# A shared SBUF region that starts at a multiple of 512 bytes instead of 64

## The chip, the core and the metric

The kernel runs on one core of a Trainium2 chip. What is measured is the time of one execution on the device, in microseconds (us).

## What is computed

Two transformer-like blocks on a 512 x 1024 float32 activation. The first has a gated MLP branch, an HGRN2 branch and a feed-forward layer; the second has two layers, each with a SwiGLU feed-forward, a mixer (attention with a pooling branch, then a short convolution) and another SwiGLU. Cut to what the change touches:

```python
x = x + mix @ w_out[l]
h = rmsnorm(x, norm_ffn[l])
x = x + jnp.square(jax.nn.relu(h @ w_ff1[l])) @ w_ff2[l]
...
mod = (c_act @ w_ada[l] + b_ada[l]).reshape(b, N_MOD, 1, D_MODEL)
...
def swiglu(h, wg, wu, wd):
    return (jax.nn.silu(h @ wg) * (h @ wu)) @ wd
```

## The kernel before

The activation is kept transposed in SBUF (`xT`, features on the 128 partitions, 512 tokens along the free dimension). Every large product runs in units of 256 output columns: SyncE loads a 1 MB panel of float32 weights into `w_raw`, ScalarE rounds it to float32r in `w_hi`, VectorE takes the rest into `w_lo`, all three with two slots. The moving operand is also split in two. Outputs of norms are in `a_hi` and `a_lo`; the hidden activations that go into a "down" product (and the mixers' outputs) are in `b_hi` and `b_lo`; the two branches of the first block leave theirs in `c_hi`, `c_lo` and `d_hi`, `d_lo`. The inner loop of such a product, the function `product`, issues three matmuls for each 128 x 128 block of weights (L622, L623, L624 in the profile), each with 512 float32r columns of the moving operand:

```python
pe.matmul(o, wh, hi[:, k, :], start=(k == ks[0]), stop=False)
pe.matmul(o, wh, lo[:, k, :], start=False, stop=False)
mm = pe.matmul(o, wl, hi[:, k, :], start=False, stop=(k == ks[-1]))
```

The function is called with `a_hi, a_lo`, with `b_hi, b_lo` (by `down` and by `hidden_group`), and with the c and d pairs (by `branches`). In the names of the profile the moving operand stands first: `po<-b_hi,w_hi` streams `b_hi` past weights from `w_hi`.

The program places every tensor by hand. `sb` gives the next free address of each partition, rounded up to 32 bytes; as the program is built, the first tensor, `xT`, is at byte 16512. The tensors that live through the whole program come first. Behind the last of them, `level_mask`, begins the region that the stages share, called `arena`. `ar` places a tensor at the arena's start plus a whole number of KB:

```python
def ar(name, shape, dt, kb):
    return sb(name, shape, dt, arena + kb * KB)
c_hi = ar("c_hi", [P, DK, S], F32R, 0)
b_hi = ar("b_hi", [P, DK, S], F32R, 48)
b_lo = ar("b_lo", [P, DK, S], F32R, 64)
```

In the arena are the b, c and d pairs, all working tensors of the HGRN2, gated MLP, attention and convolution stages (`cum`, `kk`, `qq`, `de`, `ql`, `kl`, `gv`, `qk`, `pr`, `cv` and others), the input `x_in`, and `ada_in` and `ada_acc`, which hold rows of w_ada and their running sum in the feed-forward stage of the first block. Outside it are `xT`, `w_raw`, `w_hi`, `w_lo`, `a_hi`, `a_lo`, `sq`, `stats`, `nt`, `ev`, `hid` and small tensors; the large ones of these all start at a remainder of 128 when their byte address is divided by 512.

The remainders that matter later, from adding up the sizes in the code (bytes within a partition):

| tensor | address before | mod 512 | mod 128 | address of the change | mod 512 | mod 128 |
|---|---|---|---|---|---|---|
| w_hi | 49280 | 128 | 0 | 49280 | 128 | 0 |
| a_hi | 82048 | 128 | 0 | 82048 | 128 | 0 |
| arena, c_hi | 144832 | 448 | 64 | 144896 | 0 | 0 |
| b_hi | 193984 | 448 | 64 | 194048 | 0 | 0 |
| b_lo | 210368 | 448 | 64 | 210432 | 0 | 0 |

`hi[:, k, :]` and each 128-column block of weights step in multiples of 512 bytes from the tensor's start, so a matmul's operand has the remainder of its tensor.

Each engine has its own instruction stream, and semaphores alone order them. In the feed-forward stage of the first block (`hidden_group`) VectorE also sums `ada_in` times `c_act` into `ada_acc` (L1729, L1732), squares the hidden activations into `hid` (L1764), makes `b_lo` (L1768), and adds each finished down unit to `xT` (L1777).

Of the kernel before, what the change touches and what calls it, by code (L numbers as in the profile page):

```python
# [51 lines left out]
def hybrid_two_block_kernel(  # L52
# [58 lines left out]
    with ctx:  # L111

        cursor = [(nc.sbuf_usable_end - nc.sbuf_bytes_remaining + 31) // 32 * 32]

        def sb(name, shape, dt, offset=None):
            size = {F32: 4, F32R: 4, I32: 4, U8: 1}[dt]
            for n in shape[1:]:
                size *= n
            if offset is None:
                offset = cursor[0]  # L120
                cursor[0] = (offset + size + 31) // 32 * 32
            return nc.alloc_sbuf_tensor_at(name, shape, dt, offset=offset)
# [28 lines left out]
        one_col = sb("one_col", [P, 1], F32)  # L151
        small = sb("small", [P, 64], F32)
        level_mask = sb("level_mask", [P, LV + 1, P], U8)
        arena = cursor[0]
        KB = 1024

        def ar(name, shape, dt, kb):
# [1863 lines left out]
```

## Time and profile before

| | |
|---|---|
| median of 3 runs | 2880.39 us (2879.53 to 2882.75) |
| the profiled execution, its own time | 2878.74 us |
| its span | 2876.6 us |
| TensorE (PE) busy | 2747.4 us, 96% |
| VectorE (DVE) busy | 1435.5 us, 50% |
| ScalarE (ACT) busy | 929.1 us, 32% |
| moved from and to HBM | 112 GB/s over the span |

The span is the time between the first and the last instruction of the profile. Busy times of TensorE add up matmuls whose ends are modelled and overlap; the distance between the starts of two matmuls in the timeline is the better measure of their pace.

### The profile page before, as it was taken

How to read it: one execution, taken by the hardware profiler on the slowest of the kernel's cores; microseconds unless marked ns; L12 is line 12 of the kernel's file. 1: busy time of each engine (PE TensorE's matmuls, PEld its weight loads, DVE VectorE, ACT ScalarE, POOL GpSimd, SP SyncE). 2: the span in 40 equal slices, each digit the busy share in tenths (PEclk: the TensorE clock that was granted, in tenths of full speed). 3: DMA queues.
4: the chain of work that ended last, by engine and by line, in shares of the span. 5: the costliest groups of instructions: out<-in, count | busy, mean ns of one | idle time of the engine just before them, and what ended most of it. 6: DMA issues, size and time to landing. Idle time of an engine off the chain costs nothing.

```text
span 2876.6 us, 32115 instructions
## 1 busy us (share of the span) xinstructions
PE 2747.4 (96%) x12573; PEld 2255.2 (78%) x12573; DVE 1435.5 (50%) x1561; ACT 929.1 (32%) x1087; POOL 29.0 (1%) x50
## 2 busy tenths in 40 slices
PE   7999999999999699999968999999999999999998
PEld 6888878778777488887846788887888878788887
DVE  6677553488889733325264433344333454533333
ACT  4555423332222332224343322134222332332221
POOL 0000000000000000000030000000000000000000
PEclk9999999999999899999979999999999999999999
DMA  4111222377778233232311232322323222233322
GB/s 133 60 58 59 66 88 85 97 281 278 289 297 303 85 102 95 95 99 77 100 38 44 88 102 88 102 88 88 102 88 103 88 93 97 75 104 99 102 88 73
DMA packets 252092, 323.43 MB, mean 112 GB/s; under 512 B 5622, under 2 KB 242420, under 8 KB 243828
## 3 DMA queue, kind: packets, MB, share of 16 engines
q1 hardware_dynamic: 240740, 245.51, 26.6%
q10 hardware_dynamic: 11280, 76.94, 6.8%
q8 instruction: 47, 0.77, 0.1%
q14 instruction: 25, 0.20, 0.0%
HBM read 320.34 MB, written 2.10 MB: 112 GB/s over the span
## 4 chain that ended last, share of the span: by engine, by line
PE 84%; DVE 10%; issue 2%; ACT 2%; DMA 1%; ACTq 0%; SPq 0%; DVEq 0%
PE po L622 22%; PE po L624 21%; PE po L623 21%; PE po L596 3%; PE po L601 3%; PE po L597 3%; DVE w_lo L1379 2%; DVE ada_acc L1732 2%; PE pm L742 2%; PE po L705 1%; PE po L707 1%; PE po L706 1%; DVE ada_tr L1741 1%; PE pm L655 1%; DMA ada_in<-in_w_ada_dram 1%
## 5 line engine op out<-in xcount | busy, mean ns | idle before, releaser
L1379 DVE TENSOR_TENSOR w_lo<-w_raw,w_hi 128x1024 fp32r<-128x1024 f32 x472 | 561.9, 1220 | 503.2 <-ACT w_hi L970 503.1
L970 ACT ACTIVATE w_hi<-w_raw 128x1024 fp32r<-128x1024 f32 x472 | 479.1, 1051 | 900.1 <-PE po L624 871.5
L622 PE MATMUL po<-a_hi,w_hi 128*128 128x512 f32 x1792 | 700.7, 391 | 4.1 <-DVE w_lo L1379 4.1
L624 PE MATMUL po<-a_hi,w_lo 128*128 128x512 f32 x1792 | 698.4, 390 | 0.0
L623 PE MATMUL po<-a_lo,w_hi 128*128 128x512 f32 x1792 | 698.3, 390 | 0.0
L622 PE MATMUL po<-b_hi,w_hi 128*128 128x512 f32 x1152 | 457.2, 397 | 16.8 <-DVE b_lo L1768 15.1
L624 PE MATMUL po<-b_hi,w_lo 128*128 128x512 f32 x1152 | 453.8, 394 | 0.0
L623 PE MATMUL po<-b_lo,w_hi 128*128 128x512 f32 x1152 | 451.1, 392 | 0.0
L622 PEld LDWEIGHTS po<-a_hi,w_hi 128*128 128x128 f32 x1792 | 337.1, 188 | 75.5 <-DVE w_lo L1379 4.9
L623 PEld LDWEIGHTS po<-a_lo,w_hi 128*128 128x128 f32 x1792 | 337.2, 188 | 70.7 <-issue 0.7
L624 PEld LDWEIGHTS po<-a_hi,w_lo 128*128 128x128 f32 x1792 | 337.1, 188 | 70.6
L622 PEld LDWEIGHTS po<-b_hi,w_hi 128*128 128x128 f32 x1152 | 218.3, 190 | 64.8 <-DVE b_lo L1768 16.8
L624 PEld LDWEIGHTS po<-b_hi,w_lo 128*128 128x128 f32 x1152 | 217.9, 189 | 50.7
L623 PEld LDWEIGHTS po<-b_lo,w_hi 128*128 128x128 f32 x1152 | 218.2, 189 | 48.1
L1445 DVE SCALAR_TENSOR_TENSOR xT<-po,gate,xT 128x512 f32<-128x512 f32 x112 | 81.5, 748 | 297.8 <-PE po L624 297.8
L1822 DVE TENSOR_TENSOR hid<-ev,po 128x1024 f32<-128x1024 f32 x44 | 53.7, 1221 | 274.8 <-PE po L624 274.8
L596 PE MATMUL po<-a_hi,w_hi 128*128 128x512 f32 x336 | 136.1, 405 | 24.5 <-ACT a_hi L1000 24.5
L1732 DVE SCALAR_TENSOR_TENSOR ada_acc<-ada_in,c_act,ada_acc 128x2304 f32<-128x2304 f32 x56 | 144.1, 2611 | 1.9 <-DMA ada_in<-in_w_ada_dram 1.9
L597 PE MATMUL po<-a_hi,w_lo 128*128 128x512 f32 x336 | 135.4, 403 | 0.0
L1257 ACT ACTIVATE ev<-po 128x1024 f32<-128x1024 f32 x44 | 45.2, 1027 | 217.9 <-PE po L624 217.7
L601 PE MATMUL po<-a_lo,w_hi 128*128 128x512 f32 x336 | 107.7, 403 | 0.8 <-DVE a_lo L1415 0.8
L596 PEld LDWEIGHTS po<-a_hi,w_hi 128*128 128x128 f32 x336 | 66.0, 196 | 45.0 <-issue 30.9
(251 smaller groups left out, 2469.5 us busy)
## 6 DMA issues: line engine op xcount, KB each, us to landing
ada_in<-in_w_ada_dram ACTq DMA_DIRECT2D x64, 1152.0 KB, 5.7
w_raw<-in_ffn_wg_dram SPq DMA_DIRECT2D x44, 1024.0 KB, 5.3
w_raw<-in_ffn_wu_dram SPq DMA_DIRECT2D x44, 1024.0 KB, 5.3
w_raw<-in_w_ff_dram SPq DMA_DIRECT2D x32, 1024.0 KB, 5.3
w_raw<-in_ffn_wd_dram SPq DMA_DIRECT2D x32, 1024.0 KB, 5.1
w_raw<-in_w_in_dram SPq DMA_DIRECT2D x28, 1024.0 KB, 5.1
w_raw<-in_ffn_wd_dram SPq DMA_DIRECT2D x16, 768.0 KB, 4.7
w_raw<-in_w_in_c_dram SPq DMA_DIRECT2D x12, 1024.0 KB, 5.1
```

Of the source, the lines that this page charges most:

```text
L596: pe.matmul(po[:, slot, b, :], w_hi[:, slot, c], hi[:, k, :], start=(k == 0), stop=False)
L597: pe.matmul(po[:, slot, b, :], w_lo[:, slot, c], hi[:, k, :], start=False, stop=False)
L601: mm = pe.matmul(po[:, slot, b, :], w_hi[:, slot, c], lo[:, k, :], start=False, stop=(k == kc - 1))
L622: pe.matmul(o, wh, hi[:, k, :], start=(k == ks[0]), stop=False)
L623: pe.matmul(o, wh, lo[:, k, :], start=False, stop=False)
L624: mm = pe.matmul(o, wl, hi[:, k, :], start=False, stop=(k == ks[-1]))
L742: mm = pe.matmul(out_v[:, t, :], ks, qs, start=True, stop=True)
L970: act.activation(w_hi[:, s, part], w_raw[:, s, part], ACT.Copy).then_inc(hi_done, 1)
L1379: dve.tensor_tensor(w_lo[:, s, part], w_raw[:, s, part], w_hi[:, s, part].bitcast(F32), ALU.subtract).then_inc(lo_done, 1)
L1445: ins = dve.scalar_tensor_tensor(xT[:, c, :], po[:, s, b, :], gates[:, c:c + 1], xT[:, c, :], ALU.mult, ALU.add)
L1732: ins = dve.scalar_tensor_tensor(ada_acc[:, l, :], ada_in[:, l, :], c_act[:, k:k + 1], ada_acc[:, l, :], ALU.mult, ALU.add)
L1822: dve.tensor_tensor(hid[:, :], ev[:, 0, :], po[:, 1, :, :].rearrange("p b n -> p (b n)"), ALU.mult).then_inc(out_taken[1], 2)
```

## The change

The arena's start is rounded up to a multiple of 512 bytes. It moves from 144832 to 144896, so each tensor in it moves by 64 bytes, and no tensor outside it moves. Every engine has the same instructions in the same order as before.

```diff
         small = sb("small", [P, 64], F32)
         level_mask = sb("level_mask", [P, LV + 1, P], U8)
-        arena = cursor[0]
+        LINE = 512
+        arena = (cursor[0] + LINE - 1) // LINE * LINE
         KB = 1024
```

## Rows read from the trace of the kernel before

**Rows 1.** The page: span, and busy time of each engine.
```profile
span 2876.6 us, 32115 instructions
...
PE 2747.4 (96%) x12573; PEld 2255.2 (78%) x12573; DVE 1435.5 (50%) x1561; ACT 929.1 (32%) x1087; POOL 29.0 (1%) x50
```

**Rows 2.** The page: engines' shares of the chain that ended last.
```profile
PE 84%; DVE 10%; issue 2%; ACT 2%; DMA 1%; ACTq 0%; SPq 0%; DVEq 0%
```

**Rows 3.** Groups: line, names, shapes, count | busy us, mean ns | idle before.
```profile
L622 PE MATMUL po<-a_hi,w_hi 128*128 128x512 f32 x1792 | 700.7, 391 | 4.1 <-DVE w_lo L1379 4.1
...
L622 PE MATMUL po<-b_hi,w_hi 128*128 128x512 f32 x1152 | 457.2, 397 | 16.8 <-DVE b_lo L1768 15.1 <-DVE b_lo L1913 1.7
...
L622 PE MATMUL po<-c_hi,w_hi 128*128 128x512 f32 x64 | 25.2, 394 | 0.0
...
L622 PE MATMUL po<-d_hi,w_hi 128*128 128x512 f32 x32 | 13.7, 427 | 4.7 <-DVE d_lo L1685 4.7
```

**Rows 4.** Timeline, TensorE, first and last of 240 a matmuls: start us, us.
```profile
2398.52 0.39 PE L622 MATMUL po<-a_hi,w_hi 128*128 128x512 f32 x1
...
2452.70 0.39 PE L624 MATMUL po<-a_hi,w_lo 128*128 128x512 f32 x1
```

**Rows 5.** Timeline, TensorE, first and last of 192 b matmuls.
```profile
1804.71 0.40 PE L622 MATMUL po<-b_hi,w_hi 128*128 128x512 f32 x1
...
1848.44 0.39 PE L624 MATMUL po<-b_hi,w_lo 128*128 128x512 f32 x1
```

**Rows 6.** Timeline, TensorE, first and last of 48 c matmuls.
```profile
472.85 0.40 PE L622 MATMUL po<-c_hi,w_hi 128*128 128x512 f32 x1
...
483.62 0.39 PE L624 MATMUL po<-c_hi,w_lo 128*128 128x512 f32 x1
```

**Rows 7.** L622 alone in those three stretches: length, busy (count), clock.
```profile
2398.50:2452.92 54.42, 31.12 (x80) 15.02 (x80) 1.00 0.27 90
1804.70:1848.60 43.90, 25.22 (x64) 12.00 (x64) 1.00 0.30 96
472.84:483.80 10.96, 6.31 (x16) 3.00 (x16) 1.00 0.30 96
```

**Rows 8.** Timeline, TensorE, near 355 and 730 us, while the clock is low.
```profile
354.87 0.63 PE L624 MATMUL po<-a_hi,w_lo 128*128 128x512 f32 x1
355.29 0.63 PE L622 MATMUL po<-a_hi,w_hi 128*128 128x512 f32 x1
355.72 0.63 PE L623 MATMUL po<-a_lo,w_hi 128*128 128x512 f32 x1
...
729.06 0.63 PE L622 MATMUL po<-b_hi,w_hi 128*128 128x512 f32 x1
729.49 0.63 PE L623 MATMUL po<-b_lo,w_hi 128*128 128x512 f32 x1
729.91 0.63 PE L624 MATMUL po<-b_hi,w_lo 128*128 128x512 f32 x1
```

**Rows 9.** Timeline, TensorE: products whose moving operand is 256 weight columns.
```profile
1419.78 0.28 PE L644 MATMUL po<-w_lo,a_hi 128*128 128x256 f32 x1
1419.90 0.28 PE L645 MATMUL po<-w_hi,a_lo 128*128 128x256 f32 x1
1420.02 0.28 PE L643 MATMUL po<-w_hi,a_hi 128*128 128x256 f32 x1
```

**Rows 10.** Two stretches: PE, PEld, DVE, ACT, POOL busy (count), clock, DMA, GB/s.
```profile
1595.00:1963.00 368.00, 364.92 (x1591) 299.56 (x1590) 138.36 (x137) 107.61 (x114) 0.00 (x0) 1.00 0.30 94
...
670.00:765.00 95.00, 90.91 (x397) 74.50 (x396) 81.80 (x54) 24.08 (x25) 0.00 (x0) 0.98 0.78 288
```

**Rows 11.** Timeline, TensorE and VectorE, feed-forward stage of the first block.
```profile
727.26 0.51 PE L622 MATMUL po<-b_hi,w_hi 128*128 128x512 f32 x1 [4.09 <-DVE b_lo L1768]
...
754.00 1.29 DVE L1777 TENSOR_TENSOR xT<-po,xT 128x512 f32<-128x512 f32 x2 [1.56 <-PE po L624]
...
764.89 1.29 DVE L1777 TENSOR_TENSOR xT<-po,xT 128x512 f32<-128x512 f32 x2 [2.28 <-PE po L624]
```

**Rows 12.** Groups on VectorE, outside the arena and with operands in it.
```profile
L1379 DVE TENSOR_TENSOR w_lo<-w_raw,w_hi 128x1024 fp32r<-128x1024 f32 x472 | 561.9, 1220 | 503.2 <-ACT w_hi L970 503.1
...
L1768 DVE TENSOR_TENSOR b_lo<-hid,b_hi 128x1024 fp32r<-128x1024 f32 x16 | 19.6, 1225 | 0.0
...
L1764 DVE TENSOR_TENSOR hid<-ev 128x1024 f32<-128x1024 f32 x16 | 19.6, 1225 | 27.3 <-ACT ev L1234 27.3
```

**Rows 13.** Waits of VectorE for the w_ada rows: us in total, times, longest.
```profile
DVE ada_acc L1729 <- DMA ada_in<-in_w_ada_dram: 2.1, 1, 2.1
DVE ada_acc L1732 <- DMA ada_in<-in_w_ada_dram: 1.9, 2, 1.4
```

## Prediction

> **What bounds the kernel now.** I read the page first. TensorE is busy 96% of the span [rows 1] and carries 84% of the chain that ended last [rows 2], so whatever changes the pace of its matmuls changes the end nearly one for one. The groups by line say where those matmuls are: L622 to L624 run 1792 times each on the a pair and 1152, 64 and 32 times each on the b, c and d pairs [rows 3]. The last three are in the arena, the a pair is not. They do the same work (128 x 128 weights, 512 columns), and yet the mean of one is 391 ns for a and 397 and 394 for b and c [rows 3]. That mean has a modelled end in it, so I went to the timeline and took distances between starts in unbroken stretches at the full clock.
>
> - a: 240 matmuls from 2398.52 to 2452.70 us, 54.18 / 239 = 226.7 ns each [rows 4].
> - b: 192 from 1804.71 to 1848.44, 43.73 / 191 = 229.0 ns [rows 5].
> - c: 48 from 472.85 to 483.62, 10.77 / 47 = 229.1 ns [rows 6].
>
> The counts are three times the L622 counts of the same stretches, at granted clock 1.00 in all three, with the DMA share at 0.27, 0.30 and 0.30 [rows 7]. So a matmul that streams from the arena starts 2.3 ns later than one that streams from outside. When the granted clock is at its lower level (1.2 GHz), both step by 0.43 us [rows 8]: 512 columns at 1.2 GHz are 426.7 ns, nothing is added for either. At 2.4 GHz the columns alone would be 213.3 ns; a adds 13.4 ns to that, b and c 15.7. The products with 256 moving columns step by 120 ns [rows 9], 106.7 plus 13.3. The addition is thus a fixed one for each matmul, at the full clock only, and for arena operands it is 2.3 ns larger.
>
> What distinguishes them? Not freshness: c was written long before its products, b just before, and both pay the same. Not the distance from hi to lo: 16 KB for a, b and c alike. Not the weights: the same `w_hi` and `w_lo`. What is left is the starting address: a starts at a multiple of 128 bytes (128 mod 512), b and c 64 bytes past one (448 mod 512), or else the distance between moving operand and weights (0 for a, 320 mod 512 for b and c).
>
> **The change part by part.** It removes and adds no instruction. Every arena operand moves from 448 to 0 mod 512, and so onto a multiple of 128.
>
> *Matmuls.* The affected ones are 3 x (1152 + 64 + 32) = 3744 [rows 3]. From 229.0 to a's 226.7 is 2.25 ns unrounded: 3744 x 2.25 = 8.4 us. A few dozen of them run at the low clock, and part of the d ones behind VectorE's 4.7 us of lateness [rows 3], for which I take off 0.1. That leaves 8.3 us. Where is it on the path? In the second block's feed-forwards TensorE is busy 364.9 of 368 us [rows 10], so the saving counts whole; the next thing behind a down product is the norm, which waits for it. In the first block's feed-forward the pace is shared: TensorE waits 4.09 us for `b_lo` before the down half of a group, but in that half VectorE waits for TensorE (1.56 and 2.28 us before its additions to `xT`) [rows 11], and its chain into the next group starts from the last of those. A shorter down half starts that chain earlier, so this share counts too: four groups of 192, 768 x 2.25 = 1.7 us. If it did not, the sum would be 6.6 us. Bounds for one matmul: nothing regained (0 us), or the whole 15.7 ns that stand above the columns (58.8 us), since no row shows an operand at 0 mod 512. I take the a row, the nearest: its operand too is on a 128 boundary and not on a 256 one.
>
> *VectorE and ScalarE.* A 128x1024 subtraction takes 1220 ns wholly outside the arena, 1225 with two operands in it, and 1225 for a square that is again wholly outside [rows 12]. The arena costs them nothing that I can see, so there is nothing to gain: 0 us.
>
> *DMA.* `ada_in`, `x_in` and some small tensors are landed in the arena. VectorE waits 4.0 us in all for `ada_in` [rows 13]; that bounds a gain there, and the cover for the rest is VectorE's own sums. I take 0.
>
> Sum: 8.3 us from the profiled execution's 2878.74 gives 2870.4. The median is 1.65 us above that execution, so the forecast is 2872.1 us, 0.29% faster. A measurement of this kernel can tell about 0.2% (5.8 us) from no change.
>
> **The rivals.**
>
> *No change, 18%.* The 2.3 ns belong to the distance between moving operand and weights (or to something else than the address's remainder). That distance goes from 320 to 384 mod 512 and not to 0, so the pace stays at 229.0: 2880 us, from 2878 to 2883. For it: in the trace, address and distance change together, so neither is excluded. Against it: moving columns and weights are read at different paces through a stretch, so a fixed phase between their addresses has no time at which it holds. The Trainium skill (SBUF — State Buffer, "Door 1: The DMA port swizzle") says that SBUF has 16-byte cachelines and that a penalty is paid for crossing to a new one; both starts are multiples of 16, so by that page alone nothing would change. The rows above do not agree with it, since there a and b, both multiples of 16, differ by 2.3 ns.
>
> *Much faster, 7%.* The 13.4 ns that a pays may be its own price for starting 128 bytes into a 256- or 512-byte line. Operands at 0 mod 512 would then start without it: 3744 x 15.7 = 58.8 us less, 2822 us. For it: nothing in the trace starts at 0, and the 256-column products, also at 128, pay the same. Against it: a cost that is the same for 256 and 512 columns looks just as much like that of switching to new weights.
>
> *Slower, 5%.* At 0 mod 512 the arena stream collides with the weight reads at 128 in a way that 448 did not. Place: the same 3744 matmuls. If the addition grows by as much as it was above a's, they cost 8.4 us more: 2889 us. It counts as slower from 1.6 ns a matmul (5.8 / 3744). No row speaks for it but that the pair 0 and 128 isn't in the trace.
>
> The forecast has 70%, with its own range of 2869.5 to 2875.
>
> **How the numbers follow.** The range must leave out at most 2 in 10, so it takes the forecast's case and the one without change: 2868 to 2882.5, which leaves out the two ends (12%) and a little. Faster by over 0.2%: 70% and 7%, less 3% for a forecast case that loses the shared stages and noise with them: 0.74. Within 0.2%: 18% and that 3%: 0.21. Slower: 0.05.
>
> **What would show it.** In the new trace, a b stretch of 192 matmuls should take 43.3 us from first start to last start and not 43.7, c the same pace as a, and a itself should still be at 226.7. VectorE's 1225 and 1220 ns should stand. The second block's four feed-forwards hold 2112 of the matmuls, and should give 4.7 us of the total. I am wrong if b stays at 229.0 (the remainder is not the cause), if it falls well under 226.7 (the a pair pays for its own address too), or if b is at a's pace and the span has not moved, which would mean that another engine took the time back.

## The result, and the profile after it

The changed kernel takes 2894.8 us (median of 6 runs, 2893.79 to 2896.23) against 2880.75 us for the kernel before: ratio 1.0049, 95% interval 1.0037 to 1.0061. It is 14 us slower. The prediction was 2872.1 us, 8 us faster, with a range from 2868 to 2882.5, so the time lies outside the range and on the other side. Of the runs of the kernel before that stand beside e5 to e8, one took 3115 us at a granted clock of 0.84 and is left out of the comparisons.

The page of the changed kernel, which answers to [rows 1] and [rows 2]:

```profile
span 2893.5 us, 32115 instructions
...
PE 2765.4 (96%) x12573; PEld 2256.7 (78%) x12573; DVE 1435.3 (50%) x1561; ACT 929.0 (32%) x1087; POOL 29.0 (1%) x50
...
PE 85%; DVE 10%; issue 2%; ACT 2%; DMA 1%; ACTq 0%; SPq 0%; DVEq 0%
```

TensorE alone has grown, by 18 us. VectorE and ScalarE have their old busy times to 0.2 us. The lines of the source are one further down now, so L622 is L623. Its groups in the changed kernel (columns as in [rows 3]):

```profile
L623 PE MATMUL po<-a_hi,w_hi 128*128 128x512 f32 x1792 | 700.0, 391 | 4.1 <-DVE w_lo L1380 4.1
...
L623 PE MATMUL po<-b_hi,w_hi 128*128 128x512 f32 x1152 | 460.2, 399 | 16.7 <-DVE b_lo L1769 14.7 <-DVE b_lo L1914 1.7 <-DVE w_lo L1380 0.3
...
L623 PE MATMUL po<-c_hi,w_hi 128*128 128x512 f32 x64 | 25.3, 395 | 0.0
```

The a pair stands at 391 ns as before, b has gone from 397 to 399. The timeline of the changed kernel gives the distances between starts. These are the first and the last matmul of an a stretch of 240, a b stretch of 192 and a c stretch of 48, the ones of [rows 4], [rows 5] and [rows 6]:

```profile
2412.55 0.39 PE L623 MATMUL po<-a_hi,w_hi 128*128 128x512 f32 x1
...
2466.72 0.39 PE L625 MATMUL po<-a_hi,w_lo 128*128 128x512 f32 x1
...
1815.23 0.40 PE L623 MATMUL po<-b_hi,w_hi 128*128 128x512 f32 x1
...
1859.79 0.39 PE L625 MATMUL po<-b_hi,w_lo 128*128 128x512 f32 x1
...
475.04 0.40 PE L623 MATMUL po<-c_hi,w_hi 128*128 128x512 f32 x1
...
486.00 0.39 PE L625 MATMUL po<-c_hi,w_lo 128*128 128x512 f32 x1
```

a: 54.17 / 239 = 226.7 ns, as before. b: 44.56 / 191 = 233.3 ns, and was 229.0. c: 10.96 / 47 = 233.2. So each arena matmul is about 4.3 ns slower, and 3744 x 4.3 = 16 us. That covers the 14 us of the medians; the interval of the ratio is 11 to 18 us.

Is something else touching SBUF at those moments? In the windows view of the changed kernel (columns as in [rows 10]) there is a piece of the same b stretch in which VectorE, ScalarE and GpSimd do nothing:

```profile
1841.50:1848.30 6.80, 6.80 (x31) 5.47 (x30) 0.00 (x0) 0.00 (x0) 0.00 (x0) 1.00 0.49 154
```

The matmuls inside it, from the timeline, 27 of them from first to last:

```profile
1841.82 0.40 PE L623 MATMUL po<-b_hi,w_hi 128*128 128x512 f32 x1
...
1847.89 0.40 PE L625 MATMUL po<-b_hi,w_lo 128*128 128x512 f32 x1
```

6.07 / 26 = 233.5 ns: the pace is the same with the other compute engines silent. The DMA queues are at work there (the last but one figure of the row, 0.49 of their time). In the last down product of the program they are not:

```profile
2860.00:2881.00 21.00, 21.00 (x92) 16.89 (x91) 6.22 (x8) 2.01 (x2) 0.00 (x0) 1.00 0.00 0
...
2860.22 0.40 PE L624 MATMUL po<-b_lo,w_hi 128*128 128x512 f32 x1
...
2880.99 0.39 PE L623 MATMUL po<-b_hi,w_hi 128*128 128x512 f32 x1
```

The last of these is the 90th, so 20.77 / 89 = 233.4 ns without any DMA: it is not DMA either. At the low clock level no difference shows, as before the change ([rows 8]): the step is 0.43 us.

```profile
732.77 0.63 PE L624 MATMUL po<-b_lo,w_hi 128*128 128x512 f32 x1
733.20 0.63 PE L625 MATMUL po<-b_hi,w_lo 128*128 128x512 f32 x1
733.62 0.63 PE L623 MATMUL po<-b_hi,w_hi 128*128 128x512 f32 x1
```

### The profile page after: what moved, and what is told of

Same layout as the page of the kernel before. It is cut to its first block, busy times and chain, and to the rows that moved or that the text cites. A ratio compares the mean times of both kernels' runs of the same rounds, so it can differ in the third digit from the quotient of the medians.

```text
span 2893.5 us, 32115 instructions
## 1 busy us (share of the span) xinstructions
PE 2765.4 (96%) x12573; PEld 2256.7 (78%) x12573; DVE 1435.3 (50%) x1561; ACT 929.0 (32%) x1087; POOL 29.0 (1%) x50
## 4 chain that ended last, share of the span: by engine, by line
PE 85%; DVE 10%; issue 2%; ACT 2%; DMA 1%; ACTq 0%; SPq 0%; DVEq 0%
PE po L623 22%; PE po L624 22%; PE po L625 22%; PE po L597 2%; PE po L602 2%; PE po L598 2%; PE pm L743 2%; DVE w_lo L1380 2%; DVE ada_acc L1733 2%; PE po L706 1%; PE po L708 1%; PE po L707 1%; DVE nt L1411 1%; DVE ada_tr L1742 1%; ACT ev L1235 1%
## 5 line engine op out<-in xcount | busy, mean ns | idle before, releaser
L623 PE MATMUL po<-a_hi,w_hi 128*128 128x512 f32 x1792 | 700.0, 391 | 4.1 <-DVE w_lo L1380 4.1
L623 PE MATMUL po<-b_hi,w_hi 128*128 128x512 f32 x1152 | 460.2, 399 | 16.7 <-DVE b_lo L1769 14.7
L624 PE MATMUL po<-b_lo,w_hi 128*128 128x512 f32 x1152 | 458.8, 398 | 0.0
L623 PEld LDWEIGHTS po<-a_hi,w_hi 128*128 128x128 f32 x1792 | 336.8, 188 | 76.3 <-DVE w_lo L1380 5.4
L623 PEld LDWEIGHTS po<-b_hi,w_hi 128*128 128x128 f32 x1152 | 219.0, 190 | 72.6 <-DVE b_lo L1769 16.5
```

## The experiments

Two theories stood after the result. Theory A: the operand's own address modulo 512 sets its pace (128 good, 448 middling, 0 bad). Theory R: the distance between the moving operand and the weights sets it. Below, "distance" is the address of the moving tensor less that of `w_hi`. It is 0 mod 512 for the a pair, 320 for the arena before, 384 with the change. The step or pace is always the distance between the starts of two matmuls that follow each other. All edits are against the kernel before.

**e1: everything 64 bytes further up.**

```diff
-        cursor = [(nc.sbuf_usable_end - nc.sbuf_bytes_remaining + 31) // 32 * 32]
+        cursor = [(nc.sbuf_usable_end - nc.sbuf_bytes_remaining + 31) // 32 * 32 + 64]
```

> Every tensor of the program, outside the arena too, is 64 bytes further up. The arena then starts at 0 mod 512, as in the change, and the weights and the a pair at 192; the distances between tensors are those of the kernel before. Theory A (the address of the moving operand, taken modulo 512, sets its pace): b matmuls step by 233.3 ns as in the change, and the a pair, now at 192, may leave 226.7; 2893 us or more. Theory R (the distance between moving operand and weights sets it: 0 gives 226.7, 320 gives 229.0, 384 gives 233.3): nothing moves, b at 229.0, a at 226.7, 2880.5 us.

Measured: 2879.64 us against 2880.11, ratio 0.9997 (0.9987 to 1.0006). A b stretch of 192 from its timeline:

```profile
1213.30 0.40 PE L622 MATMUL po<-b_hi,w_hi 128*128 128x512 f32 x1
...
1257.04 0.39 PE L624 MATMUL po<-b_hi,w_lo 128*128 128x512 f32 x1
```

43.74 / 191 = 229.0 ns, though the arena is at the very address that it has in the changed kernel. The a pair, now at 192 mod 512, still has 226.7. Theory A falls: neither pair pays for the address that it has here.

**e2: only the arena, to distance 0.**

```diff
-        arena = cursor[0]
+        arena = cursor[0] + 192
```

> Only the arena moves, by 192 bytes: it starts at 128 mod 512 like all large tensors outside it, so address and distance to the weights are both those of the a pair (distance 0 mod 512). Theories A and R both expect b, c and d at 226.7 ns and a median 8 us below the kernel before, near 2872 us. Theory H (what lies above some address, as 128 KB, is slower, and the low bits only change by how much): b stays above 229.

Measured: 2870.4 us (11 runs), ratio 0.9971 (0.9962 to 0.998). The b stretch:

```profile
1203.31 0.39 PE L622 MATMUL po<-b_hi,w_hi 128*128 128x512 f32 x1
...
1246.61 0.39 PE L624 MATMUL po<-b_hi,w_lo 128*128 128x512 f32 x1
```

43.30 / 191 = 226.7 ns, the pace of a. The gain that had been forecast for the change is here, at another address.

**e3 and e4: pieces of the arena at different distances.** The b, c and d pairs are each shifted by their own amount; the lists give the first KB of a piece and its shift.

```diff
+        SHIFT = [(0, 128), (32, 256), (48, 384)]      # e3
+        SHIFT = [(0, 96), (32, 320), (48, 448)]       # e4
...
-            return sb(name, shape, dt, arena + kb * KB)
+            extra = [s for first, s in SHIFT if kb >= first][-1]
+            return sb(name, shape, dt, arena + kb * KB + extra)
```

> Three pieces of the arena are shifted by different amounts: the c pair by 128 bytes (64 mod 512, distance to the weights 448), the d pair by 256 (192, distance 64), the b pair by 384 (320, distance 192). Theory R expects c to be no better than 229, since the three known distances 0, 320, 384 give 226.7, 229.0 and 233.3, and cannot say more; theory A expects the b pair, whose remainder is 64 mod 128 as before, at 229.0, and c and d, both 64 mod 128 too, at 229.0.

> Three pieces of the arena are shifted by different amounts: the c pair by 96 bytes (32 mod 512, distance to the weights 416), the d pair by 320 (256, distance 128), the b pair by 448 (384, distance 256). Theory A in the form that only a multiple of 256 is bad: d 233.3, b near 226.7. Theory R: unknown distances; if the cost grows with the distance up to a wrap, d 227 to 228, b 228 to 229, c over 233.

Measured, one execution each: 2893.23 and 2880.14 us. b stretches of 192 in e3, then in e4, and a c stretch of 48 in e4:

```profile
1211.60 0.39 PE L624 MATMUL po<-b_hi,w_hi 128*128 128x512 f32 x1
...
1256.17 0.39 PE L626 MATMUL po<-b_hi,w_lo 128*128 128x512 f32 x1
```

```profile
1210.47 0.39 PE L624 MATMUL po<-b_hi,w_hi 128*128 128x512 f32 x1
...
1253.76 0.39 PE L626 MATMUL po<-b_hi,w_lo 128*128 128x512 f32 x1
...
399.44 0.40 PE L624 MATMUL po<-c_hi,w_hi 128*128 128x512 f32 x1
...
410.44 0.40 PE L626 MATMUL po<-c_hi,w_lo 128*128 128x512 f32 x1
```

That is 233.4 ns for b in e3 (distance 192), 226.7 for b in e4 (256) and 234.0 for c in e4 (416, 234.2 over all its stretches); worked out in the same way from the traces, c in e3 (448) has 233.3, d in e3 (64) 229.6 and d in e4 (128) 233.2. My guess of a cost that grows with the distance up to a wrap at 512 missed: 256 is as good as 0, 448 is the same as 192, 384 as 128, and 320 as 64 (d had 229.6 at 320 too, in e1). The period is 256 bytes.

The time of e4 does not show what its pace shows: 3456 b matmuls that are each 2.3 ns faster are worth 8 us, and yet it took 2880.14 us. Its granted clock was 0.976, where the profiled execution of the kernel before had 0.978; over 2878 us that is worth some 6 us (an estimate from those two figures). In e2 too, the three executions at 0.975 and 0.976 took 2873.4 to 2878.2 us and the other eight 2868.1 to 2871.1. A single execution says less here than the steps in its trace.

**e5: only the weights move.** A gap of 64 bytes before `w_hi`, and 448 behind `w_lo`, so that all that follows keeps its remainder.

```diff
+        cursor[0] += 64
         w_hi = sb("w_hi", [P, 2, UNIT], F32R)
         w_lo = sb("w_lo", [P, 2, UNIT], F32R)
+        cursor[0] += 448
         a_hi = sb("a_hi", [P, DK, S], F32R)
```

> Only the two weight buffers w_hi and w_lo move by 64 bytes against everything else (what lies behind them moves by 512, which leaves its remainder alone). Distance of the moving operand to the weights, mod 256: a pair 192 instead of 0, arena 0 instead of 64. Theory R (distance to the weights, with period 256): the two change places, the b, c and d matmuls at 226.7 ns and the a ones at 233.3; as more matmuls use the a pair (over 5400 of L622 to L624 and some 1500 elsewhere), the time rises to 2910 to 2920 us. Theory O (it is the distance to some other tensor outside the arena that engines or DMA touch meanwhile): both stay where they were, a at 226.7 and b at 229.0, 2880 us.

Measured: 2905.72 us, one execution. A b stretch of 192 and an a stretch of 288:

```profile
1212.02 0.39 PE L624 MATMUL po<-b_hi,w_hi 128*128 128x512 f32 x1
...
1255.33 0.39 PE L626 MATMUL po<-b_hi,w_lo 128*128 128x512 f32 x1
...
1255.56 0.39 PE L624 MATMUL po<-a_hi,w_hi 128*128 128x512 f32 x1
...
1322.52 0.39 PE L626 MATMUL po<-a_hi,w_lo 128*128 128x512 f32 x1
```

b 43.31 / 191 = 226.8 ns, a 66.96 / 287 = 233.3; c has 227.1 and d 227.6. Only the weights have moved modulo 512, and the slow pair is now the fast one. This settles that the partner is the weight buffers. The time rose by 25 us and not by 30 to 40. I had counted every a matmul as bounding. The first block's feed-forward has 768 of them, and yet it is no longer than before, 383.7 us against 386.4 from its first matmul to the next norm's. Its granted clock was 0.98 there and 0.97 before, which is worth a few us; what else hides the slower matmuls was not followed.

The second thing I had miscounted is the form with 256 columns ([rows 9]), in which the weights stream and the a pair is loaded. In e5 its distance, moving less loaded, goes from 0 to 64. The same 143 matmuls in the kernel before and then in e5, first and last:

```profile
1413.67 0.28 PE L644 MATMUL po<-w_lo,a_hi 128*128 128x256 f32 x1
...
1430.70 0.28 PE L645 MATMUL po<-w_hi,a_lo 128*128 128x256 f32 x1
```

```profile
1419.88 0.28 PE L646 MATMUL po<-w_lo,a_hi 128*128 128x256 f32 x1
...
1435.98 0.28 PE L647 MATMUL po<-w_hi,a_lo 128*128 128x256 f32 x1
```

17.03 / 142 = 119.9 ns before, 16.10 / 142 = 113.4 in e5: they became faster by leaving distance 0. A stretch of 96 near the start of the program went from 119.9 to 117.8. In e1, where weights and a pair move together, both stretches are at their old pace. So distance 0 is the best of those tried for the 512-column form alone, and not for this one.

**e6: `w_lo` moves against `w_hi`, and `b_lo` against `b_hi`.** The a, c and d pairs and `b_hi` are at distance 0 to `w_hi` and 192 to `w_lo`, `b_lo` at 64 and 0. `ar` adds the shift as in e3.

```diff
+        cursor[0] += 64
         w_lo = sb("w_lo", [P, 2, UNIT], F32R)
+        cursor[0] += 192
         a_hi = sb("a_hi", [P, DK, S], F32R)
...
-        arena = cursor[0]
+        arena = cursor[0] + 192
+        SHIFT = [(0, 0), (64, 64)]
```

> Only w_lo moves by 64 bytes against w_hi, and in the b pair b_lo by 64 against b_hi. Mod 512: w_hi 128, w_lo 192; a, c, d pairs and b_hi 128 mod 256, b_lo 192 mod 256. Theory N (what counts is the distance between the operand that streams and the weights that are being loaded meanwhile for the next matmul: hi streams while w_hi is loaded, lo streams while w_lo is loaded): all b distances are 0, so b at 226.7 ns; a has one bad distance of three (192), so 226.7 + 6.7/3 = 228.9. Theory P (distance to the matmul's own weights): a 228.9 too, but b has 64 for lo with w_hi and 192 for hi with w_lo, so 226.7 + (2.3 + 6.7)/3 = 229.7.

Measured: 2909.53 us, one execution. The b stretch, 44.14 / 191 = 231.1 ns:

```profile
1214.19 0.39 PE L626 MATMUL po<-b_hi,w_hi 128*128 128x512 f32 x1
...
1258.33 0.39 PE L628 MATMUL po<-b_hi,w_lo 128*128 128x512 f32 x1
```

a has 231.1 too. c has 231.0 and d 230.9, so all four pairs have one pace, although `b_lo` stands at other distances than the rest. Neither theory holds: N wanted 226.7 for b, P 229.7, and both wanted 228.9 for a.

**e7: three more distances**, with `SHIFT = [(0, 32), (32, 160), (48, 224)]`.

> The arena's pieces at three distances to the weights not yet measured: the c pair 96, the d pair 224, the b pair 32 mod 256. By the distances measured so far (0: 226.7, 64: 229.0, 128: 233.3, 160: 234.2, 192: 233.3 ns) I expect 231 for 96, 229 to 230 for 224, and 227.5 for 32, if the curve is smooth; a curve in steps of 64 bytes would give 32 the pace of 0 or of 64. Time 2875 to 2881 us.

Measured: 2895.02 us, one execution. From the trace: 96 has 233.6 ns, 224 has 233.4, 32 has 233.4. The expected 231, 229 to 230 and 227.5 all missed, and so did the time. The curve is not smooth. Of the multiples of 32, for the 512-column form, only 0 adds nothing to the 226.7 ns, 64 adds 2.3 to 2.9, and the other six add 6.5 to 7.5.

**e8: both the first tensor and the arena at a multiple of 256.**

```diff
-        cursor = [(nc.sbuf_usable_end - nc.sbuf_bytes_remaining + 31) // 32 * 32]
+        cursor = [(nc.sbuf_usable_end - nc.sbuf_bytes_remaining + 255) // 256 * 256]
...
-        arena = cursor[0]
+        arena = (cursor[0] + 255) // 256 * 256
```

> The first tensor and the arena both start at a multiple of 256 bytes, so weights, a pair and arena operands all have remainder 0 mod 256 (256 mod 512), and all distances are 0. Theory R: as with the arena moved by 192, every product at 226.7 ns and 2871 us. Theory A2 (a remainder of 0 mod 256 is bad by itself, for a stream or for a landing DMA): a, b and c all slower, over 2880 us.

Measured: 2869.89 us (5 runs), ratio 0.9963 (0.9949 to 0.9977). b, c, d and a step by 226.7 ns; a b stretch of 192, 43.30 / 191:

```profile
1206.38 0.39 PE L622 MATMUL po<-b_hi,w_hi 128*128 128x512 f32 x1
...
1249.68 0.39 PE L624 MATMUL po<-b_hi,w_lo 128*128 128x512 f32 x1
```

A remainder of 0 mod 256 is harmless once the weights have it too. This version is faster than both kernels, level with e2.

**e9: hi and lo of a pair at different distances**, with `arena = cursor[0] + 192` and `SHIFT = [(0, 0), (16, 128), (40, 256), (64, 320)]`.

> The arena starts at distance 0 to the weights, and hi and lo of a pair are then put at different distances (mod 256): c pair hi 0, lo 128; d pair hi 128, lo 0; b pair hi 0, lo 64. In each three matmuls hi streams twice and lo once. If each matmul pays for its own distance alone: c 226.7 + 6.7/3 = 228.9 ns, d 226.7 + 2 x 6.7/3 = 231.1, b 226.7 + 2.3/3 = 227.4. If one bad distance disturbs the neighbours too, as the 231.1 of the kernel with w_lo moved by 64 suggests (228.9 was expected there), all three come out 1 to 3 ns above these.

Measured: 2888.18 us, one execution. The b stretch of 192, and a c stretch of 48:

```profile
1209.43 0.39 PE L624 MATMUL po<-b_hi,w_hi 128*128 128x512 f32 x1
...
1253.74 0.39 PE L626 MATMUL po<-b_hi,w_lo 128*128 128x512 f32 x1
...
397.14 0.39 PE L624 MATMUL po<-c_hi,w_hi 128*128 128x512 f32 x1
...
407.90 0.39 PE L626 MATMUL po<-c_hi,w_lo 128*128 128x512 f32 x1
```

b (0 and 64) 232.0 ns, c (0 and 128) 228.9, d (128 and 0) 229.0. Only c is what adding up gives. A 64 that costs 2.3 ns when all three matmuls share it costs 5.3 on average when one of three has it. So the prices don't add up matmul by matmul. The expectation that all three come out 1 to 3 ns higher fell for each: c is at the sum, d is 2.1 ns below it and b 4.6 above it.

## Why the prediction was wrong

**What bounds the kernel** was right. TensorE's pace sets the end, arena matmuls had a price of 2.3 ns at the full clock and none at the low one, and 3744 of them are touched. VectorE, ScalarE and DMA gave nothing that shows in the total, as forecast: VectorE's subtraction is at 1225 ns still, and its waits for `ada_in` came to 1.9 us where they had been 4.0.

**The step that failed** is the price after the change: "I take the a row, the nearest: its operand too is on a 128 boundary and not on a 256 one". I had reduced the candidates to two, the address and the distance to the weights, and took the address. e1 has the changed kernel's arena address with 229.0 ns, and e5 swaps the paces of a and b by moving the weights alone, so it is the distance. With the change that distance went from 64 to 128 mod 256, and the price from 2.3 to 6.6 ns. The size of the sum follows at once: 3744 x 4.3 = 16 us more, where I had 8.3 less. My list of signs of being wrong had b at 229.0 or below; a b that gets slower stood only among the rivals.

**The argument against the distance** was that columns and weights are read at different paces, so that no phase between them can last. It was reasoning without a row behind it, and it cost the most: it turned an open question of two candidates into 70 to 18. e1 to e5 show that the distance sets the pace through whole stretches, whatever the two reads do within one.

**The rivals.** "No change" had the right partner, the weights, and then assumed that 384 costs what 320 does. "Slower" had the right place, the right partner and the right sign, with 5%, because no row spoke for a pair of 0 and 128; its 8.4 us, against 14 measured, took the size of the addition from another distance. But no row spoke for that pair being free either. "Much faster" did not happen: at remainder 0 mod 256 (256 mod 512) with all distances 0 (e8) a matmul still takes 226.7 ns, and an arena at 0 mod 512 with the old distance (e1) is at its old pace, so no run shows the 13.4 ns above the columns to be a price of starting at 128. The prediction also called that addition a fixed one for each matmul. In e5 a 256-column matmul adds 6.7 ns to its 106.7 where it had added 13.2, so it is not fixed. By the 16-byte cachelines that the Trainium skill states (SBUF — State Buffer, "Door 1: The DMA port swizzle") nothing would have changed here; the runs show 226.7 to 234 ns among starts that are all multiples of 16 bytes.

**The share on the path** was right within what these runs can tell: e2 gains 9.7 us at the medians (the interval is 6 to 11), where 8.4 less 0.1 was worked out for that pace. The 1.7 us of it that were put in the first block's feed-forward can't be checked by themselves: from its first matmul to the next norm's it takes 385.7 us in e2 and 386.4 before, a difference that one execution of each doesn't settle.

**Still open** is the mechanism inside the engine. Each matmul is paired with a weight load that overlaps it, the effect shows at the full clock only, neither other compute engines nor DMA need be active, and a common shift does nothing. A conflict between TensorE's two readings of SBUF fits all of that, but was not isolated: no run had a stream without weight loads. e6 and e9 show paces for mixed distances that no rule of mine gives, and why the 256-column form gains by distance 64 is open too. The bytes between multiples of 32 were not tried.

## What to carry to other kernels

Before aligning one buffer, ask what it has to be aligned with: here the 512-column moving operands should start at the same remainder mod 256 as the weights that they stream past, and the round number of the start is worth nothing in itself. For another form of matmul the best distance may be another, as the 256-column one shows; measure its step first. When two operands of the same instruction have slightly different paces, list all that differs between them, and if two candidates change together, predict both outcomes of the edit under each before choosing. A price found in a trace at one value says nothing on a value that the trace doesn't hold; it may be worse than all that it does.

## What the runs showed of the hardware

- In this kernel, a float32r matmul with 512 moving columns, in a stream of such matmuls, starts every 226.7 ns at the full clock if moving operand and weights have the same remainder mod 256 (227.1 and 227.6 in the short c and d stretches of e5). At a distance of 64 the step is 229.0 to 229.6, at 32, 96, 128, 160, 192 and 224 it is 233.2 to 234.2: up to 3.3% of such a matmul's step for where a buffer lies.
- With 256 moving columns, weights streaming, the step was 119.9 ns at distance 0 and 113.4 and 117.8 at 64 (e5).
- The distance counts, not the address: with 64 bytes on everything the 95% interval of the ratio is 0.9987 to 1.0006 (e1).
- The period is 256 bytes: 0 and 256, 64 and 320, 128 and 384, 192 and 448 each have one pace.
- At the low clock level no difference shows (a step of 0.43 us in both kernels).
